# Eight attention heads as one interleaved pipeline over three token pieces

## The reference, cut to what matters

```
q = rmsnorm(rope(c_q  @ w_q[h]))           # 96 = 64 + 32 rotary
k = rmsnorm([rope(k_rope), c_kv @ w_k[h]])
v = c_kv @ w_v[h]                          # 64
s = (q @ k.T) / sqrt(96), causal
o = softmax(s) @ v ;  o *= silu(z)[h]
```

## Time and profile before

| | us |
|---|---|
| median of three runs | 3545.39 |
| span of the profiled execution | 3557.2 |
| PE busy, share of span | 3139.6, 88% |
| DVE busy | 1569.9, 44% |
| ACT busy | 711.5, 20% |
| POOL busy | 833.7, 23% |
| granted TensorE clock, mean | 0.929 |

### The profile page before, as it was taken

One profiled execution on the slowest core, in us unless ns is written; L12 is line 12 of the kernel. 1 busy time (PEld: TensorE's weight loads), 2 busy tenths in 40 slices (PEclk: granted clock), 3 DMA queues, 4 the chain that ended last, 5 costly groups with the idle time before them and its releaser, 6 DMA issues.

```text
span 3557.2 us, 40295 instructions
## 1 busy us (share of the span) xinstructions
PE 3139.6 (88%) x16640; PEld 2803.0 (79%) x16640; DVE 1569.9 (44%) x1540; ACT 711.5 (20%) x1191; POOL 833.7 (23%) x646
## 2 busy tenths in 40 slices
PE   6975676999999995999997888898999997888899
PEld 4754565777777774999997787798999997877789
DVE  4677456333333336500115665663520114655671
ACT  2132310000000002000112454400000111544410
POOL 2321012233333331333322000022333332000012
PEclk9987789999999997999998888899999998988899
DMA  2100011111111111112112000042112112000131
GB/s 98 47 30 27 0 71 38 47 46 43 47 47 41 47 47 66 54 42 96 48 42 77 8 13 13 31 152 94 42 48 90 48 42 84 13 13 7 37 145 71
DMA packets 46201, 182.47 MB, mean 51 GB/s; under 512 B 5744, under 2 KB 5872, under 8 KB 45552
## 3 DMA queue, kind: packets, MB, share of 16 engines
q1 hardware_dynamic: 31248, 113.19, 10.0%
q10 hardware_dynamic: 14816, 67.28, 4.9%
HBM read 150.06 MB, written 30.39 MB: 51 GB/s over the span
## 4 chain that ended last, share of the span: by engine, by line
PE 70%; DVE 20%; ACT 4%; issue 3%; DMA 1%; POOL 1%; DVEq 0%; ACTq 0%; SPq 0%; POOLq 0%
PE acc L353 61%; PE aux L648 2%; DVE act_lo L1214 2%; DVE ff_split L1214 2%; DVE small L1665 2%; DVE ff_split L1213 1%; DVE residual L1279 1%; PE acc L629 1%; PE acc L613 1%; DVE act_hi L1213 1%; DVE work L1230 1%; DMA spill_g<-work 1%; DVE work L1223 1%; ACT pool_split L1146 1%; PE aux L686 1%
## 5 line engine op out<-in xcount | busy, mean ns | idle before, releaser
L353 PE MATMUL acc<-act_hi,w_hi 128*128 128x348 f32 (+1 forms) x3488 | 868.4, 351 | 106.0 <-DVE act_lo L1214 39.2
L353 PE MATMUL acc<-act_lo,w_hi 128*128 128x348 f32 (+1 forms) x3488 | 855.7, 347 | 0.0
L353 PE MATMUL acc<-act_hi,w_lo 128*128 128x348 f32 (+1 forms) x3488 | 853.0, 346 | 0.0
L353 PEld LDWEIGHTS acc<-act_hi,w_hi 128*128 128x128 f32 x3488 | 619.3, 193 | 168.1 <-issue 70.5
L321 POOL TENSOR_TENSOR small<-shape_consts 128x1 f32<-128x1 f32 x212 | 47.1, 222 | 2666.4 <-PE acc L353 2666.4
L353 PEld LDWEIGHTS acc<-act_lo,w_hi 128*128 128x128 f32 x3488 | 624.4, 193 | 44.0
L353 PEld LDWEIGHTS acc<-act_hi,w_lo 128*128 128x128 f32 x3488 | 620.8, 192 | 42.1
L324 POOL TENSOR_TENSOR w_lo<-w_raw,w_hi 128x1024 fp32r<-128x1024 f32 x212 | 568.1, 2680 | 17.0
L353 PE MATMUL acc<-ff_split,w_hi 128*128 128x512 f32 (+1 forms) x1408 | 356.6, 379 | 22.0 <-DVE ff_split L1214 22.0
L1431 DVE TENSOR_TENSOR residual<-acc,residual 128x1024 f32<-128x1024 f32 (+1 forms) x88 | 108.1, 1229 | 468.2 <-PE acc L353 468.2
L353 PEld LDWEIGHTS acc<-ff_split,w_hi 128*128 128x128 f32 x1408 | 257.6, 190 | 71.1 <-DVE ff_split L1214 26.5
(11 more groups left out here) (215 smaller groups left out, 2887.3 us busy)
## 6 DMA issues: line engine op xcount, KB each, us to landing
w_raw<-in_wstream SPq DMA_DIRECT2D x215, 512.0 KB, 3.5
spill_x<-residual ACTq DMA_DIRECT2D x2, 4176.0 KB, 12.7
spill_m<-residual ACTq DMA_DIRECT2D x2, 4176.0 KB, 13.2
spill_g<-work ACTq DMA_DIRECT2D x2, 4176.0 KB, 14.3
residual<-spill_m ACTq DMA_DIRECT2D x16, 522.0 KB, 5.9
work<-spill_g ACTq DMA_DIRECT2D x16, 522.0 KB, 7.9
residual<-spill_x ACTq DMA_DIRECT2D x16, 522.0 KB, 4.3
residual<-in_xT ACTq DMA_DIRECT2D x8, 512.0 KB, 9.9
```

The lines of the kernel that those rows point to most:

```text
L353: ins = nc.tensor.matmul(acc[0:m, s, p, 0:w], wt[:, ws, w0 + j * m:w0 + j * m + m], x[:, k, p * w:p * w + w], start=(first and t == 0), st ...
```

## The change

The phases over all tokens are replaced by one loop of 15 steps per head on every engine, run for h = -1 to 7 with g = h+1. In step n, TensorE does block n of the scores of head h and weighs block n-2; between them it does a share of the preparation of head g, now cut into token pieces of 384, 384 and 276: the projections (one or two chunks a step), one of the sums, rough scores, a turn of the maxima. Rough scores of query blocks 6 to 8 of head h fall in its own steps 1 to 4. All counters become explicit numbers (`wave`, `block_no`, `rough_no`).

PSUM is dealt out anew: one bank each for query projection, key and value projection, sums and turned values, rough scores; two for score blocks; two for the weighed values. Values' operands exist twice (for two heads); probability buffers hold four blocks, and the float32 copy lies in the place of the low part. The key, query and norm buffers are pieces of 384 columns, two of each.

The subtraction that makes the low part of a probability block moves from VectorE to GpSimd (`low_values`, 15 a head). GpSimd splits the weight unit of head h+2 after block 2 of head h, instead of at once when the slot is free. VectorE keeps the low parts of keys, queries and values. Its constants fill twice as many value tiles, and the wait for `spill_g` now stands ahead of all its work for the heads.

In the diff below short conditions are joined with what they guard on one line.

```diff
-        PRING = 5
-        prob32 = (R[:, 18, 0:PW], R[:, 18, PW:2 * PW], extra[:, 0:PW])
+        PRING = 4
+        def prob32(k):
+            o = 8 * RW + ring0 + QP * (2 * (k % PRING) + 1)
+            return R_[:, o:o + QP]
+        acc_q, acc_k, acc_n = (acc[:, 0, i, :] for i in range(3))
+        acc_s, acc_r = (acc[:, 1, 0, :], acc[:, 1, 1, :]), acc[:, 1, 2, :]
...
@@ gpsimd
+            def low_values(l, h, n):
+                k = block_no(l, h, n)
+                w = block_width(n)
+                pool.wait_ge(sems["p_hi"], k)
+                nc.gpsimd.tensor_tensor(prob(k, 1)[:, 0:w], prob32(k)[:, 0:w], prob(k, 0)[:, 0:w].bitcast(F32),
+                                        ALU.subtract).then_inc(sems["p_lo"], 1)
+                for h in range(-1, MH):
+                    for n in range(NB):
+                        if h >= 0:
+                            low_values(l, h, n)
+                            if n == 2:
+                                split(heads + 2 + h, ...)
@@ tensor (head_key_value, head_query, head_sum, head_values and the phases of a head go)
+                def scores(h, n):
+                    if k > 2:
+                        pe.wait_ge(sems["p_hi"], k - 2)
+                    if tiles[0][0] == 0:
+                        pe.wait_ge(sems["max_row"], wave(l, h, pc))
+                        pe.wait_ge(sems["k_lo"], wave(l, h, pc))
+                        pe.wait_ge(sems["q_lo"], wave(l, h, pc))
...
+                for h in range(-1, MH):
+                    g = h + 1
+                    more = g < MH
+                    for n in range(NB):
+                        if h >= 0:
+                            scores(h, n)
+                            if n == 0:
+                                turn_maxima(h, 1)
+                            if n in (1, 2, 3):
+                                rough_scores(h, 5 + n, 0)
+                            if n == 4:
+                                rough_scores(h, 8, 2)
+                            if n == 5:
+                                turn_maxima(h, 2)
+                        if more:
+                            if n in (8, 9, 10):
+                                rough_scores(g, n - 8, 0)
+                            if n == 11:
+                                turn_maxima(g, 0)
+                            if n in (12, 13, 14):
+                                rough_scores(g, n - 9, 0)
+                            if n in (0, 4, 8):
+                                key_value_part(g, n // 4)
+                            elif n < 12:
+                                query_part(g, n // 4, n % 4 - 1)
+                            if n in (3, 7, 11):
+                                key_sum(g, n // 4)
+                            if n in (4, 8, 12):
+                                query_sum(g, n // 4 - 1)
+                            if n in (6, 10, 13):
+                                turn_values(g, (n - 6) // 3)
+                            if n in (13, 14):
+                                rough_scores(g, n - 9, 1)
+                        if h >= 0 and n in (1, 2, 3):
+                            rough_scores(h, 5 + n, 1)
+                        if h >= 0 and n >= 2:
+                            weigh_values(h, n - 2)
+                        if h >= 1 and n < 2:
+                            weigh_values(h - 1, NB - 2 + n)
@@ scalar
+                        if h >= 0:
+                            exponents(h, n)
+                            if n == 0: maximum_row(h, 1)
+                            if n == 2 and h >= 1: inverse_sums(h - 1, 2)
+                            if n == 4: inverse_sums(h, 0)
+                            if n == 5: maximum_row(h, 2)
+                            if n == 9: inverse_sums(h, 1)
+                        if more:
+                            if n == 11: maximum_row(g, 0)
+                            if n in (4, 8, 12): key_scale(g, n // 4 - 1)
+                            if n in (0, 4, 8): key_value_evict(g, n // 4)
+                            if n in (5, 9, 13): query_scale(g, n // 4 - 1)
+                            if n in (7, 11, 14): high_values(g, (n - 7) // 3)
+                            if n in (3, 7, 11): query_squares(g, n // 4)
@@ vector
+                        if h >= 0:
+                            if n == 3 and h >= 1: head_out(h - 1, 2)
+                            if n in (1, 2, 3): maximum(h, 5 + n, 0); maximum(h, 5 + n, 1)
+                            if n == 4: maximum(h, 8, 2); maxima_of(2)
+                            if n == 5: head_out(h, 0)
+                            if n == 10: head_out(h, 1)
+                        if more:
+                            if n in (4, 8, 12): query_table(g, n // 4 - 1)
+                            if n in (5, 9, 13): key_norm(g, n // 4 - 1)
+                            if n in (6, 10, 14): query_norm(g, (n - 6) // 4)
+                            if n in (7, 11): low_part_values(g, (n - 7) // 4)
+                            if n in (8, 9, 10): maximum(g, n - 8, 0)
+                            if n in (12, 13, 14): maximum(g, n - 9, 0)
+                            if n in (13, 14): maximum(g, n - 9, 1)
+                            if n == 14: maxima_of(1); low_part_values(g, 2)
```

More of the change, by code:

```diff
@@ new lines, in key_sum @@
+                def key_sum(g, pc):
+                    k = wave(l, g, pc)
+                    c0, w = QP * pc, piece_width(pc)
+                    if n_free[0] is not None:
+                        pe.wait_ge(*n_free[0])
+                    pe.wait_ge(sems["k_squared"], k)
+                    nc.tensor.matmul(acc_n[:, 0:w], ones96, X[:, 6, c0:c0 + w], start=True,
+                                     stop=True).then_inc(sems["k_sum"], 1)
+                    n_free[0] = (sems["kn_free"], k)
@@ new lines, in turn_maxima @@
+                def turn_maxima(h, pc):
+                    pe.wait_ge(*r_free[0])
+                    if pc:
+                        pe.wait_ge(sems["max_ready"], 2 * (l * MH + h) + pc)
+                    for i in range(3 * pc, 3 * pc + 3):
+                        n = min(P, TP - P * i)
+                        o = P * (i - 3 * pc)
+                        ins = nc.tensor.matmul(acc_r[32:33, o:o + n], S_[:, 16 + i:17 + i], ident[:, P - n:P],
+                                               start=True, stop=True)
+                    ins.then_inc(sems["max_turned"], 1)
+                    r_free[0] = (sems["max_row"], wave(l, h, pc))
@@ L622, in scores_t @@
                     at = 0
-                    for j, lo, w in BLOCKS[n][1]:
-                        out = acc[:, s, b, at:at + w]
+                    for j, lo, w in tiles:
+                        out = acc_s[k % 2][:, at:at + w]
                         at += w
@@ L1723, in _ @@
-                low_parts(4)
-                head_out(MH - 1, 1)
+                for h in range(-1, MH):
+                    g = h + 1
+                    more = g < MH
+                    for n in range(NB):
+                        if h >= 0:
+                            if n == 3 and h >= 1:
+                                head_out(h - 1, 2)
+                            if n in (1, 2, 3):
+                                maximum(h, 5 + n, 0)
+                                maximum(h, 5 + n, 1)
+                            if n == 4:
+                                maximum(h, 8, 2)
+                                maxima_of(2)
+                            if n == 5:
+                                head_out(h, 0)
+                            if n == 10:
+                                head_out(h, 1)
+                            if n in (6, 8) and not more:
+                                j = n // 2 - 3
+                                split(X[:, j, :], Fy[0][:, j, wide], Fy[1][:, j, wide], "f_ready")
+                        if more:
+                            if n in (4, 8, 12):
+                                query_table(g, n // 4 - 1)
+                            if n in (5, 9, 13):
+                                key_norm(g, n // 4 - 1)
+                            if n in (6, 10, 14):
+                                query_norm(g, (n - 6) // 4)
+                            if n in (7, 11):
+                                low_part_values(g, (n - 7) // 4)
+                            if n in (8, 9, 10):
+                                maximum(g, n - 8, 0)
+                            if n in (12, 13, 14):
+                                maximum(g, n - 9, 0)
+                            if n in (13, 14):
+                                maximum(g, n - 9, 1)
+                            if n == 14:
+                                maxima_of(1)
+                                low_part_values(g, 2)
```

659 lines of the change are left out of this document (336 added, 323 removed).

## The result

The changed kernel takes 3575.31 us (median of four runs, 3575.05 to 3576.18), the kernel before 3546.71 beside it (3545.22 to 3548.24): ratio 1.009, 95% interval 1.0076 to 1.0104. It is 28.6 us slower; 3507 us (3455 to 3570), faster than before, was forecast.

What follows compares the result with a forecast made beforehand. TensorE, neither free nor at its best, loses time to waits and half clock. A head of 48 us gives layers of 50.8 + 7 x 48 + 22.5 = 409.3 against 428.4, 38 less for two: 3507 us, range 3455 to 3570.

Steps and rivals of the forecast that it cites:

- The clock: Steady head, from step 11: one drop of 6.8 us at half clock, half inside waits, adding 2 us; bounds 0 and 5.
- the walk: One steady head followed through all engine queues with measured durations: 46 us at full clock, 8.0 of them TensorE waiting.
- TensorE's own work: Steady head: TensorE's products priced at full clock sum to 38.4 us, taken as 38; the head can't be shorter.
- The waits: TensorE idle in steps 4, 7, 8, 11, 12, 13 and 14 of a steady head, 8.0 us in sum.
- step 11: Turned maxima wait 2.2 us for VectorE's maximum behind key_norm, head_out and query_norm; then key_sum waits 0.5.
- step 4: query_sum waits for the bank that key_scale frees, behind ScalarE's exponents and inverse: 1.6 us idle.
- Contention: GpSimd's low parts beside VectorE: 0.8 us twice in steps 9 to 14, inside the 8.0; bounds nothing or 3 us more.
- The rival that put 3 us on it: VectorE and GpSimd block each other in steps 9 to 14, with more half clock: head 52.5, 3570 us; chance 0.15.
- The start: Before head 0, VectorE waits for the spill ahead of its first query_table: 50.8 us against 43.8; bounds 45 and 54.
- Head 7: Last head, without projection: 19 us of TensorE work and two blocks to drain, 22.5 us against 26.2 (20 to 25).
- The sum's base: Profiled span forecast at 3519 us; the median taken 11.8 below the span, as before, giving 3507.
- it wins nothing: Rival: two clock drops as before and the longer start eats the rest; head 50.5, 3542 us; chance 0.11.

Runs made afterwards that it cites:

- e1_fill: Changed kernel plus 26 matmuls of 384 columns a head without a use, ahead of TensorE's waits in steps 4, 11, 12, 13 and 14; 3527.30 us.
- e6: Kernel before the change plus 24 matmuls of 384 columns a head without a use, ahead of its own three waits; 3495.66 us, ratio 0.9849.
- e9_fill_no_low: Changed kernel plus 26 matmuls a head without a use, with GpSimd's low parts cut to one column; 3548.23 us.
- e4: Changed kernel with key_scale ahead of the inverse sums in step 4 and the maximum ahead of head_out in step 10; 3510.24 us, ratio 0.9897.
- e7: Changed kernel with VectorE's first query_table ahead of its wait for the spill; 3558.88 us.
- e11_best: Changed kernel with order swapped in steps 4 and 10, first query_table before the spill wait, 17 useless matmuls a head and 30 before head 0; 3486.93 us.

## Why the prediction was wrong, by its own steps

The forecast for a layer was 50.8 + 7 x 48 + 22.5 = 409.3; it is 51.7 + 7 x 51.07 + 29.7 = 438.9 (first scores of head 0 at 1941.33, head 7 from 2298.8). The 29.6 are 0.9 in the start, 21.5 in the seven heads and 7.2 in head 7.

- **The clock (the failed step).** I gave it 2 us a head, from one drop of 6.8 half inside the waits. There were 10.2 us of half clock, mostly outside the waits. By TensorE's busy time they cost 4.2 us a head (44.74 against 40.5 in e1_fill); taking them away gave 3.75 (51.25 to 47.5), the fillers being a little longer than the idle time that they filled. The bound of 5 was right, the value was not. What misled me: I charged the drop to steps 11 to 14, where it begins. Its second half lands on the full steps after them, and there it costs all of its length. Nor did I ask the question of the kernel before: its own 13.7 us of half clock were worth 4.7 us a head (51.2 to 46.5 in e6), so the head to be beaten at full clock was one of 46.5, and the walk's 46 was hardly a gain over it.
- **TensorE's own work (wrong by 2.5 a head, and again in head 7).** 38 us were forecast; 40.5 were measured at full clock, and 39.4 for the old order, which I took as 0.4 below the new one. In which products the 2.5 lie, no run shows.
- **The waits (right in place, 1.5 too long).** 8.0 us were forecast, 6.5 measured; step 11 has 1.75 of 2.2, step 4 has 1.35 of 1.6. So the 46 at full clock came out near 47.0 by two errors against each other. And the row of the kernel before already said that the waits were no gain: its idle time was 51.2 - 45.05 = 6.15 us, less than the 8.0 that I gave to the new order. All of the forecast gain rested on the clock and on work priced too low.
- **Contention (small in the steady heads, by luck of place).** TensorE waited 3.1 us in the whole program for a low part, all in the two heads 7. The longest low part took 1.78 us, over the 1.5 that I had named as the sign of large contention, and it is one of 276 columns that takes 0.77 alone; it too stands in head 7. `key_norm`'s last part has a mean of 559 ns over its 14. Stretched were `query_norm`'s rounding L1784 (619 ns for 360 alone), the copy L1772 (557 for 350) and the first product of `head_out` (812 ns for 276 columns, 440 alone); none of them stood in front of TensorE. In e9_fill_no_low one was, at 1.2 us a head. The rival that put 3 us on it named a possible price and the wrong place.
- **The start (right within 1 us, in part by luck).** 50.8 was forecast, 51.7 came. TensorE stood in step 5 behind the spill as worked out, but was let go 27.2 us after the first product where I had 28.9, and needed 24.5 from there where I had 21.9. That this start is 7 to 8 us longer than the old 43.8 was in the forecast; the heads were to pay for it and did not. It is 7.9 us longer in the first layer and 7.7 in the second, 15.6 of the 18 us that the two layers cost more.
- **Head 7 (wrong by 7.2).** I took it as 19 us of work and 3.5 of waits at full clock. Measured at full clock (e1_fill) it is 22.6 of work and 4.9 of waits, and its half clock in the changed kernel adds 2.2. The waits are 3.2 us for VectorE's maximum, since rough blocks have one bank instead of two slots and no projection stands between them, and 1.6 for the last low parts. That the one bank costs this is shown by the rows alone; no run undid it.
- **The sum's base.** I carried 11.8 us, from the profiled run of before to its median, over to the new kernel. The new kernel's profile lies 1.9 below its median. These 13.7, less 4.5 in the rest of the span (2.6 of them the late window of the earlier trace rows), and some 59 of the two layers (29.6 and 29.3) are the 68 us between 3507 and 3575.

The nearest rival was "it wins nothing": its head of 50.5 came within 0.8 us and its clock drops came true (two, of 3.4 and 6.8 us), and its 3542 fell short by the heads, head 7 and the base. Where the expected gain went, per steady head: the changed order has 1.1 us more of work (40.5 against 39.4), 0.4 more idle time (6.5 against 6.15) and 1.4 less for the clock (4.2 against 5.6). It did remove idle time at the changes of phase, but put as much into steps that were full before. The loss itself is in the start, and in the first layer in head 7 (3.5 us) as well. Open is why both kernels have a head of 51.2 us to 0.1; edits that move the drops (e4, e7 in its first layer) change the period by 1.5 to 3.5 us at once.

## What to carry to other kernels

Before you price a new order, hold the clock in both orders: a few matmuls without a use ahead of each wait show in one run what a head costs at most at 2.4 GHz (here 46.5 before and 47.5 after, both with some filler time on the path), and they may be the gain by themselves (1.5% for 24 of them a head). Then look at the waits: two swaps in the order of ScalarE's and VectorE's lists gave 65 us here, more than 26 fillers a head. Compare idle time with idle time before you trust a walk: the rows of the kernel before held 6.15 us where the walk of the new one had 8.0. Price start and end of a pipeline by themselves; here they are the loss. Charge a drop of the clock to the work that stands behind the idle place, at its whole length. Short GpSimd instructions beside VectorE were cheap here, where none that they stretched stood before TensorE in a steady head; a wide one must be kept from the VectorE instruction that TensorE waits for.

## What the runs showed of the hardware

- Behind idle places of 0.9 to 1.8 us, with busy matmuls between them, stood 3.4 and 6.8 us at 1.2 GHz in every head; with 17 matmuls of 384 columns in them and the order of e4 (e11_best) all steady heads ran at 2.4 GHz.
- The run-to-run spread of a kernel on one core can be that of its clock: 3534 to 3563 us for the kernel before at mean clocks of 0.937 to 0.929, 3500 to 3528 for e4_order at 0.953 to 0.943, but 1.2 us for the changed one at 0.936 to 0.937, and 2.5 for e11_best, whose clock does not fall in the heads.
- A VectorE product with two inputs from SBUF took 2.44 us beside a GpSimd subtraction of 2.38 and 0.79 beside a GpSimd rounding of 1.04; one of GpSimd's low parts took 1.78 where 0.77 is its time alone, beside VectorE's splits.
